# Expert tiles of a mixture-of-experts layer: the row gather moved one tile ahead, its transposes ahead of the down products, and the middle loop unrolled into nested conditions

## The reference

```python
for each expert block (128 rows in the reference):
    hmid = x @ w_up[e] + b_up[e]                    # 1024 -> 2048
    hg = minimum(hmid[:, :1024], 7); hl = clip(hmid[:, 1024:], -7, 7)
    act = hg * sigmoid(1.702 * hg) * (hl + 1)
    y = act @ w_down[e] + b_down[e]                 # 1024 -> 1024
out[token] += gate * y
```

## Time and profile before

| | |
|---|---|
| median of three runs | 1563.44 us (1560.44 to 1568.46) |
| span of the profiled execution | 1565.7 us; it lies among the three times, and no other time of its own is given |
| TensorE busy / weight loads busy | 1300.1 us (83%) / 697.0 us (45%) |
| VectorE, ScalarE, GpSimd busy | 530.9, 209.8, 225.4 us |
| moved by DMA | 480.52 MB, mean 307 GB/s |
| mean granted clock of TensorE | 0.928 |
| the experts' stage | from 554 us (first bias product) to the end |

### The profile page before, as it was taken

One profiled execution on the slowest core, in us unless ns is written; L12 is line 12 of the kernel. 1 busy time (PEld: TensorE's weight loads), 2 busy tenths in 40 slices (PEclk: granted clock), 3 DMA queues, 4 the chain that ended last, 5 costly groups with the idle time before them and its releaser, 6 DMA issues.

```text
span 1565.7 us, 30929 instructions
## 1 busy us (share of the span) xinstructions
PE 1300.1 (83%) x11087; PEld 697.0 (45%) x11088; DVE 530.9 (34%) x1344; ACT 209.8 (13%) x561; POOL 225.4 (14%) x349
## 2 busy tenths in 40 slices
PE   7999999999898977669998996695796886857865
PEld 5778777778786532223443332231232332312322
DVE  2999756643573251111211111111111111111155
ACT  2111232414240210000000000000000000000001
POOL 2008700124220010000100000000010000001320
PEclk9999999999999998779999997898898998978987
DMA  7586455204037789999978999999999999999996
GB/s 186 125 267 158 101 128 143 86 9 109 1 119 230 279 364 419 420 410 416 419 290 357 405 417 418 419 419 416 419 419 417 406 390 412 418 417 419 418 372 237
DMA packets 147329, 480.52 MB, mean 307 GB/s; under 512 B 15438, under 2 KB 76118, under 8 KB 114471
## 3 DMA queue, kind: packets, MB, share of 16 engines
q1 hardware_dynamic: 135695, 463.37, 77.3%
q0 software_dynamic: 2560, 10.29, 1.6%
q10 hardware_dynamic: 9024, 6.17, 1.2%
HBM read 462.42 MB, written 18.21 MB: 307 GB/s over the span
## 4 chain that ended last, share of the span: by engine, by line
PE 59%; DMA 17%; DVE 8%; issue 6%; SPq 3%; POOL 3%; ACT 2%; DVEq 1%; POOLq 0%
PE bank L1287 17%; DMA arena<-in_w_up 16%; PE bank L1299 10%; PE bank L782 9%; PE bank L1255 5%; PE bank L1273 3%; DVE acc L1826 3%; PE bank L1174 2%; PE bank L1182 2%; PE bank L865 2%; POOL acc L548 2%; SPq L447 2%; SPq L450 1%; PE bank L1082 1%; POOL temps L545 1%
## 5 line engine op out<-in xcount | busy, mean ns | idle before, releaser
L1287 PE MATMUL bank<-arena,gate 128*32 128x512 f32 x3264 | 420.0, 643 | 125.4 <-DMA arena<-in_w_up 124.8
L1287 PEld LDWEIGHTS bank<-arena,gate 128*32 128x32 f32 x3264 | 103.9, 113 | 395.8 <-issue 270.7
L782 PE MATMUL bank<-arena 128*128 128x304 f32 (+1 forms) x1024 | 263.9, 420 | 3.7 <-DMA arena<-in_w_in 2.2
L2368 DVE COPY gate<-bank 128x256 f32<-128x256 f32 x46 | 19.6, 425 | 634.9 <-PE bank L1299 634.9
L782 PEld LDWEIGHTS bank<-arena 128*128 128x128 f32 x1024 | 196.9, 193 | 68.2 <-ACT zs L1497 3.1
L1299 PE MATMUL bank<-arena,gate 128*32 128x256 f32 x3264 | 190.5, 384 | 30.9 <-ACT gate L1717 29.3
L1299 PEld LDWEIGHTS bank<-arena,gate 128*32 128x32 f32 x3264 | 112.4, 111 | 96.7 <-issue 27.1
L1826 DVE SCALAR_TENSOR_TENSOR acc<-arena,pcol,acc x240 | 126.3, 609 | 0.1
L672 POOL TENSOR_TENSOR qkv<-qkv 128x192 f32<-128x192 f32 x46 | 29.4, 639 | 613.3 <-DVE qkv L2312 613.3
L1273 PE MATMUL bank<-qkv 128*128 128x512 f32 x102 | 59.5, 666 | 49.9 <-DVE gate L2354 23.4
L1255 PE MATMUL bank<-qkv 128*32 128x256 f32 (+1 forms) x1224 | 87.2, 401 | 2.0 <-POOL qkv L675 1.2
(11 more groups left out here) (424 smaller groups left out, 1169.7 us busy)
## 6 DMA issues: line engine op xcount, KB each, us to landing
arena<-in_w_up SPq DMA_DIRECT2D x256, 1024.0 KB, 12.7
arena<-in_w_down SPq DMA_DIRECT2D x256, 512.0 KB, 8.6
arena<-in_w_in SPq DMA_DIRECT2D x32, 1024.0 KB, 10.4
y_d<-gate ACTq DMA_DIRECT2D x188, 32.0 KB, 4.9
y_d<-gate POOLq DMA_DIRECT2D x1, 4608.0 KB, 28.3
arena<-in_w_conf_out SPq DMA_DIRECT2D x4, 1024.0 KB, 5.1
arena<-in_state_dn_S SPq DMA_DIRECT2D x8, 512.0 KB, 7.3
arena<-in_w_dn_out SPq DMA_DIRECT2D x1, 4096.0 KB, 15.2
```

What stands on the lines that cost most here:

```text
L782: last = mm(bank[2 * (j % 2) + f][:, 0:cols.stop - cols.start], wring[:, slot, k, P * half:P * (half + 1)], rhs[:, k, cols], start=(k == 0 ...
L1287: last = mm(hidden(q)[v], xgT[:, i, SL * q0:SL * (q0 + 1)], parts(wup[k], q)[v], start=False, stop=(k == KC - 1), skip_group_check=True)
```

## The change

- TensorE's step gathers the rows of tile b+2 at its end, where it gathered tile b+1 after the first half of up. The transposes of the rows of tile b+1 stand ahead of down, beside those of the activations, and go to the second half of bank 6, which down and take_y use too: hence a wait for y_ready ahead of them. ahead of the loop, tile 2 is gathered as well.
- ScalarE's step is copy_actt, store_y, sigmoid, copy_xg(b + 2) in that order.
- The head loop runs to tile 22 (HEAD = 23), MID becomes 5 and EXTRA 7. The inner loop goes: EXTRA copies of the step are written out, each under a condition nested in the one before, so that the first that fails skips all that are left. Passes 0 to 3 do five tiles (pass 0: tiles 23 to 27), pass 4 four.
- The two loops on TensorE, ScalarE, VectorE and GpSimd carry a hint for their back edge. SyncE's loop stays as it was.
- In the last four tiles the same order holds; match stays behind activate there.

```diff
-HEAD = NE // 2
+HEAD = 23
...
+        xgt_bank = bank[6][:, W:2 * W]
...
             def tile_step(b):
                 up_bias(b)
                 up(b, range(0, 4), now_in)
-                gather(b + 1)
                 turn(act_h, bank[4], s["act_ready"], b, s["actt_done"])
+                if not first(prev):
+                    pe.wait_ge(s["y_ready"], prev)
+                turn(xg, xgt_bank, s["xg_copied"], b + 2, s["xgt_done"])
                 down(prev, range(KC), prev_in)
                 up(b, range(4, KC), now_in)
-                turn(xg, bank[0][:, W:2 * W], s["xg_copied"], b + 2, s["xgt_done"])
+                gather(b + 2)
...
-            turn(xg, bank[0][:, W:2 * W], s["xg_copied"], 2, s["xgt_done"])
+            turn(xg, xgt_bank, s["xg_copied"], 2, s["xgt_done"])
+            gather(2)
             pe.wait_ge(s["tab_ready"], 1)
             tile_step(1)
-            with pe.Fori(2, HEAD) as b:
+            with nc.Fori(2, HEAD, engines=[pe.engine], hint_back_edge=True) as b:
                 tile_step(b)
...
-            with pe.Fori(0, MID) as i:
-                b = pe.value_load(info_i[0:1, bass.ds(i + O_MID, 1)], min_val=0, max_val=XB + MID) + HEAD
+            with nc.Fori(0, MID, engines=[pe.engine], hint_back_edge=True) as i:
+                b = pe.value_load(info_i[0:1, bass.ds(i + O_MID, 1)], min_val=0, max_val=(MID - 1) * (1 + EXTRA)) + HEAD
                 tile_step(b)
-                with pe.Fori(0, EXTRA) as j:
-                    with pe.If(i + j * MID < nx):
+                with ExitStack() as more:
+                    for j in range(EXTRA):
+                        more.enter_context(pe.If(i + j * MID < nx))
                         tile_step(b + j + 1)
             for i in range(LAST):
...
                 up(b, range(0, 4), now_in)
-                if i < LAST - 1:
-                    gather(b + 1)
                 turn_choice(i)
                 turn(act_h, bank[4], s["act_ready"], b, s["actt_done"])
+                if i < LAST - 1:
+                    pe.wait_ge(s["y_ready"], prev)
+                    turn(xg, xgt_bank, s["xg_copied"], b + 2, s["xgt_done"])
                 down(prev, range(KC), prev_in)
...
-                if i < LAST - 1:
-                    turn(xg, bank[0][:, W:2 * W], s["xg_copied"], b + 2, s["xgt_done"])
+                if i < LAST - 2:
+                    gather(b + 2)
...
             def tile_step(b):
-                copy_xg(b + 1)
                 copy_actt(b - 1)
+                store_y(b - 1)
                 sigmoid(b)
-                store_y(b - 1)
+                copy_xg(b + 2)
```

More of the change, by code:

```diff
@@ L705, in _ @@
             selected(1)
-            with pool.Fori(2, HEAD) as b:
+            with nc.Fori(2, HEAD, engines=[pool.engine], hint_back_edge=True) as b:
                 choose(b)
@@ L1737, in _ @@
             sigmoid(0)
+            copy_xg(2)
             tile_step(1)
-            with act.Fori(2, HEAD) as b:
+            with nc.Fori(2, HEAD, engines=[act.engine], hint_back_edge=True) as b:
                 tile_step(b)
             nx = act.value_load(info_i[0:1, 0:1], min_val=0, max_val=XB)
-            with act.Fori(0, MID) as i:
-                b = act.value_load(info_i[0:1, bass.ds(i + O_MID, 1)], min_val=0, max_val=XB + MID) + HEAD
+            with nc.Fori(0, MID, engines=[act.engine], hint_back_edge=True) as i:
+                b = act.value_load(info_i[0:1, bass.ds(i + O_MID, 1)], min_val=0, max_val=(MID - 1) * (1 + EXTRA)) + HEAD
                 tile_step(b)
-                with act.Fori(0, EXTRA) as j:
-                    with act.If(i + j * MID < nx):
+                with ExitStack() as more:
+                    for j in range(EXTRA):
+                        more.enter_context(act.If(i + j * MID < nx))
                         tile_step(b + j + 1)
@@ L1754, in _ @@
                 copy_actt(nx + (NE - LAST + i - 1))
-                sigmoid(b)
                 if i == 0:
                     store_y(nx + (NE - LAST - 1))
+                sigmoid(b)
+                if i < LAST - 2:
+                    copy_xg(b + 2)
             copy_actt(nx + (NE - 1))
@@ L2377, in _ @@
             tile_step(1)
-            with dve.Fori(2, HEAD) as b:
+            with nc.Fori(2, HEAD, engines=[dve.engine], hint_back_edge=True) as b:
                 tile_step(b)
@@ L2382, in _ @@
             nx = dve.value_load(info_i[0:1, 0:1], min_val=0, max_val=XB)
-            with dve.Fori(0, MID) as i:
-                b = dve.value_load(info_i[0:1, bass.ds(i + O_MID, 1)], min_val=0, max_val=XB + MID) + HEAD
+            with nc.Fori(0, MID, engines=[dve.engine], hint_back_edge=True) as i:
+                b = dve.value_load(info_i[0:1, bass.ds(i + O_MID, 1)], min_val=0, max_val=(MID - 1) * (1 + EXTRA)) + HEAD
                 tile_step(b)
-                with dve.Fori(0, EXTRA) as j:
-                    with dve.If(i + j * MID < nx):
+                with ExitStack() as more:
+                    for j in range(EXTRA):
+                        more.enter_context(dve.If(i + j * MID < nx))
                         tile_step(b + j + 1)
```

15 lines of the change are left out of this document (7 added, 8 removed).

## The result

The changed kernel takes 1620.77 us (median of four runs, 1616.39 to 1623.1) where the kernel before takes 1563.62: the measured ratio is 1.0353, with a 95% interval of 1.0326 to 1.0380 (the two medians alone give 1.0366). It is slower by 57 us between the medians. The forecast was 1557.1 us, with a range of 1550 to 1571.

A forecast was written before the change was run, and what follows sets the result against it. The weight stream (DMA near 418 GB/s) was taken as the bound, so only its standstills could be won. Terms -0.5 - 7.3 + 2.4 - 3.9 + 2 + 1 = -6.3 us took 1563.4 to 1557.1 us, range 1550 to 1571.

The forecast's parts named there:

- Third tile: At expert 8's third tile, the shorter step narrows the weight stream's hole: -0.5 us (between 0 and -1).
- old exit: Head loop's exit no longer falls between two-tile experts at TensorE's pace, so the stream's standstill there goes: -7.3 us.
- The stretch at 1250: Around 1250 us, moved pass ends of the middle loop remove the weight stream's standstill: -3.9 us.
- New exit: Head loop's exit between tiles 22 and 23, partly covered by expert 13's down chunks: +2.4 us (0 to +5.7).
- 3 us just fit in the 3.1 left: At middle-loop pass ends, the jump's instruction fetch takes 3 us and fits the slack after a two-tile expert.
- +2 for all passes: Middle-loop pass ends together, with the slow clock after a pause: +2 us (0 to +8).
- two fetches in a row: Rival: at pass ends both jump and back edge fetch, 6 us instead of 3, 15 in all; 1570 us, chance 0.18.
- The rule of the Trainium skill: TensorE holds 2048 instructions; eight copies would not fit, so jump and back edge would both stall. Set against the change.
- The tail: Last four tiles: gathers wait some 4 us for pmat, in exchange gathers leave the way of down: +1 us net (-2 to +4).
- Ahead of the loops: gather(2) waits some 4 us for pmat, covered by the stream loading expert 1's up chunks: 0.
- The step: TensorE's step in the loops shortens by 0.95 us, from 14.93 to 13.98, with nothing lost in the loops.
- a step above 14.5: Sign of being wrong: a step over 14.5 us would mean the gather waits for pmat in the loops.

The follow-up runs named there:

- copies4: The changed kernel with HEAD = 16, so four copies in the middle loop instead of eight: 1587.0 us, ratio 1.0124.
- copies7: The changed kernel with HEAD = 21, which gives six copies in the middle loop, hints kept: 1579.95 us (one run).
- inner_loop: The changed kernel with the old inner loop (middle loop of two copies), hints kept: 1588.61 us, ratio 1.0149.
- no_hint: The changed kernel without the back-edge hints of the head and middle loops: 1630.2 us, ratio 1.0423.
- middle_hint: The changed kernel with the back-edge hint in the middle loop alone: 1612.32 us, ratio 1.0320.
- fixed6: The changed kernel with HEAD = 20 (six copies), no hints, tile 2 gathered as before, match ahead of activate in the last four tiles: 1596.8 us, ratio 1.0215.
- order_fixed: The kernel before with the new order, but tile 2 gathered as before and match ahead of activate in the last four tiles: 1566.08 us, ratio 0.9992.
- order_only: The kernel before with the change's new order on TensorE and ScalarE, old loops, no hints: 1578.71 us, ratio 1.0076.
- best22: The changed kernel with HEAD = 22 (seven copies), middle-loop hint only, tile 2 gathered as before, match ahead of activate in last four tiles: 1568.59 us, ratio 1.0012.
- inner_no_hint: The changed kernel with the old two-copy inner loop and no hints in either loop: 1586.5 us, ratio 1.0119.

## Why the prediction was wrong, by its own steps

**Third tile, -0.5, and old exit, -7.3:** the exit is right, at -7.2. The third tile measured -0.7, which one pair of traces can't tell from chance (the old order alone spreads over 1.2 us); the mean of all traces says -1.1, while the step became shorter by less than half of what this term was worked out from (below). So its nearness is partly luck.

**The stretch at 1250, -3.9:** right in kind, and never seen in the changed kernel, since a fetch ahead of tile 38 fell into it. In copies4 and copies7, whose later pass ends pause 1.8 us, expert 23 comes 3.5 us earlier than before; in inner_loop, whose pass ends pause 4.1, it doesn't.

**New exit, +2.4 (0 to +5.7):** measured +10.0, outside its bounds. Without the head loop's hint the pause is 3.8 to 4.5 us and expert 14 costs about +5 (no_hint, middle_hint), twice my value; the other 5 us are a fetch at the exit. I costed the hints at nothing and named no work that hides them. They were the one part of the change with no row of the trace behind it, and deserved bounds as such.

**"3 us just fit in the 3.1 left", +2 for all passes:** this step failed, and it is half of the miss of 57 us: the pass ends cost 32 us (experts 17, 20, 23 and 26). I rightly had eleven packets of code, a target that isn't there and a slack of some 3 us, but a single fetch of 3 us. Each fetch took 5.4 to 6.3 us in the changed kernel, and two came in a row. My two bounds were zero and 4.9 us, the time to landing of a 32 KB store, and the true value lay above the upper one; I then chose the middle by a packet's time instead of the row nearest in kind, a DMA in the same full queues. The rival "two fetches in a row", with a chance of 0.18, was the true mechanism, at 6 us for both where it was 11.7, hence its 15 us in all where the table has 32. The argument against it, that the hint could bring both at once, had no row either. The slack was right: a pass end that is followed by a one-tile expert (tile 28) lost 1.2 us with 13 us of pause, the three others 8 to 12.

**The rule of the Trainium skill** that the prediction set beside this (Runtime: NRT & Kernel Launch, "Instruction fetch mechanics") had the sign and the places: jump and back edge both stalled. Its 2048 instructions are eight blocks of 256. By an estimate from the matmul records and weight loads of a tile (316), five tiles are 1580 instructions, some 6.2 blocks, and four are 4.9, each with the block of the closing branches and one fetched ahead to be added. With the hint the runs agree with that figure: by this count four tiles need 6.9 blocks and stay, five need 8.2 and miss. Without it they don't: four tiles miss in fixed6 and three stay.

**The tail, +1 (-2 to +4):** the waits for pmat were foreseen at 4 us each and measured 4.7 and 3.7, and the mended order gives back 8.9 us in order_fixed. That the weights of the last experts come only 1.3 us later is near what I put, but by luck: experts 29 to 31 take 110.7 to 121.2 us in the nine kernels with this tail, against 109.5 before, and in order_only, where only the order differs, they cost 4.9, above my bound. The 4.7 us at the end were not foreseen. VectorE stands still for 5.54 us there, for 5.0 in middle_hint and for 3.8 in best22, and for over 1 us in the last 35 us of no other kernel; a packet of the second instruction queue (q14, 8 KB) starts inside the gap, at 1587.6. So it too seems to wait for a block, though no run shows that this queue is VectorE's.

**Ahead of the loops, 0:** wrong by 6.7 us, in the sign of the cover. I wrote that the stream has expert 1's up chunks to load meanwhile; but its down chunks wait for down(0), which stands behind that gather. SyncE issues them from 586.01 us (line 452), where it did from 575.39 before (line 450):

```profile
586.01 5.40 SPq L452 DMA_DIRECT2D arena<-in_w_down  x8
...
575.39 4.91 SPq L450 DMA_DIRECT2D arena<-in_w_down  x8
```

The load that is late is the one that the waiting engine itself releases.

**The step:** this failed too, at no cost. Forecast were 13.98 us; tile 9 took 14.70, and tile 8, which waits for a chunk, 15.9. Before, tile 9 took 15.12 (the 14.93 of the prediction are tile 20's, in the middle loop), so 0.42 us went and not 0.95. The prediction named a step above 14.5 as the sign that the gather waits for pmat in the loops; the sign came, but the gather doesn't wait there. What is left are 0.6 us ahead of each bias, which the profile puts to VectorE; but VectorE's instruction (L2369) ends at 744.53 and the sequencer's last register instruction at 745.0, so it is the table reads of the next tile, no longer hidden by turn and clamp.

```profile
729.15 1.12 PE L1276 MATMUL bank<-qkv 128*128 128x512 f32 x2 [0.67 <-DVE gate L2369]
...
745.06 1.12 PE L1276 MATMUL bank<-qkv 128*128 128x512 f32 x2 [0.59 <-DVE gate L2369]
```

It cost nothing where the stream sets the pace.

Left open: why expert 0 landed 2.7 us later in the changed kernel. It landed at 520.0 to 523.9 us in the kernels with short loops and at 523.5 to 528.3 in those with copies, though nothing changed ahead of it.

## What to carry to other kernels

Before a loop body is copied out, count the instructions that one pass runs on the busiest engine, not those that are written, and compare with the longest pass that the trace shows without instruction packets. Where the packets don't stop after the first pass, each jump past them is a wait of its own. And place what can't be avoided (a loop's exit, the first jump over code that never ran) ahead of work that waits for something else anyway: the same pause of 13 us cost 1.2 us at one pass end (tile 28) and 11.7 at the next (tile 33).

An edit with no row behind it, such as a hint, is costed from both sides like any other. Here it had both signs: in the middle loop it saved 15 us, and at the head loop's exit it cost 7.

## What the runs showed of the hardware

- With the DMA queues full of weights, a jump to a block that is not on TensorE took 5.9 to 6.8 us, and a branch back 5.4 to 5.8 with the hint and 4.7 to 7.5 without, against 0.2 us where the block is there. No run has such a fetch with idle queues, so what the full queues add to it stays open.
- The engine begins behind such a pause at the lower of its clock levels (granted 0.50, that is 1.2 GHz, also in 1190 to 1195 us, where the bias product starts), and the bias product takes 2.07 us instead of 1.12. The window of the changed kernel in such a pause, columns as above:

```profile
1185.00:1190.00 5.00, 0.00 (x0) 0.00 (x0) 0.00 (x0) 0.00 (x0) 0.00 (x0) 0.50 1.01 419
```

- A condition in the inner loop that fails costs 0.8 us of TensorE's sequencer (inner_loop). Nested, the first that fails skips the rest, and a pass end costs 1.8 us instead of 2.6 to 4.2.
- A hint of the back edge in a loop whose code stays on the engine pushed its exit from 3.8 to 10.3 us (inner_no_hint, inner_loop), and did next to nothing in the kernel before (4.85 to 5.08).
- A loop pass that runs five copies of the step (some 1580 instructions) no longer finds its first block at the branch back (best22: 5.65 us); one that runs four does (0.23 us) with the hint, and one that runs three without.
